# Two moves in VectorE's order: the running sum of squares in the gated unit, and the weight splits in the attention loop

## The reference, cut to what matters

```python
x = x + 0.5 * swiglu(rmsnorm(x, ffn_norm[0, 0]), ...)
h = rmsnorm(x, mix_norm[0])
# S5: scan over time, y = gelu(C s + d u), then the gated unit:
m = (y @ w_glu_v) * sigmoid(y @ w_glu_g)
x = x + m
x = x + 0.5 * swiglu(rmsnorm(x, ffn_norm[0, 1]), ...)
c, kpe = shared_kv(x, pos, ...)
x = x + 0.5 * swiglu(rmsnorm(x, ffn_norm[1, 0]), ...)
# latent attention, 16 heads, causal over the prompt; new tokens over the paged cache
s = q_lat @ c.T + q_pe @ kpe.T
p = softmax(mask(scale * s))
x = x + (heads(p @ c) @ w_uv) @ w_o
x = x + 0.5 * swiglu(rmsnorm(x, ffn_norm[1, 1]), ...)
```

## Time and profile before

| what | us |
|---|---|
| median of 3 runs | 2173.57 |
| lowest and highest | 2173.57 and 2175.39 |
| the profiled execution | 2175.88 |
| its span in the trace | 2173.9 |
| TensorE busy in the span | 2110.8 |
| VectorE busy in the span | 1065.8 |
| ScalarE busy in the span | 736.1 |

### The profile page before, as it was taken

One profiled execution on the slowest core, in us unless ns is written; L12 is line 12 of the kernel. 1 busy time (PEld: TensorE's weight loads), 2 busy tenths in 40 slices (PEclk: granted clock), 3 DMA queues, 4 the chain that ended last, 5 costly groups with the idle time before them and its releaser, 6 DMA issues.

```text
span 2173.9 us, 46399 instructions
## 1 busy us (share of the span) xinstructions
PE 2110.8 (97%) x19638; PEld 2016.3 (93%) x19638; DVE 1065.8 (49%) x1550; ACT 736.1 (34%) x1057; POOL 145.3 (7%) x246
## 2 busy tenths in 40 slices
PE   8999999998999999999999999998988999999998
PEld 7999999987999999999999999996656799999998
DVE  5453586685455454333545543345753335545422
ACT  4221232344243443223323222244543234343211
POOL 3002002030000000000000000000036100000000
PEclk9999999999999999999999999998989899999999
DMA  7232233101323323333333333221147323232332
GB/s 149 84 106 74 86 88 101 51 10 39 96 81 87 96 87 90 101 92 81 93 92 92 87 102 94 86 93 44 43 117 209 101 61 95 87 96 87 103 91 80
DMA packets 365138, 193.07 MB, mean 89 GB/s; under 512 B 42220, under 2 KB 359658, under 8 KB 365010
## 3 DMA queue, kind: packets, MB, share of 16 engines
q1 hardware_dynamic: 357952, 180.72, 29.4%
q0 software_dynamic: 5488, 9.03, 1.5%
q10 hardware_dynamic: 1570, 1.48, 0.3%
HBM read 184.23 MB, written 3.02 MB: 86 GB/s over the span
## 4 chain that ended last, share of the span: by engine, by line
PE 89%; DVE 4%; ACT 2%; SPq 2%; issue 2%; DMA 1%; ACTq 0%; DVEq 0%
PE ps L1881 76%; PE ps L1894 2%; PE ps L2428 1%; PE ps L2326 1%; PE ps L2228 1%; PE ps L2580 1%; PE ps L2459 1%; SPq L452 1%; PE ps L2200 1%; DVE wl L1222 1%; PE ps L2405 1%; SPq L454 1%; PE ps L2217 1%; DMA cb<-cache_ckv 1%; DVE stmp L482 0%
## 5 line engine op out<-in xcount | busy, mean ns | idle before, releaser
L1881 PE MATMUL ps<-xh,wh 128*128 128x260 f32 x3232 | 847.8, 283 | 6.6 <-DVE wl L1222 4.0
L1881 PE MATMUL ps<-xl,wh 128*128 128x260 f32 x3232 | 842.1, 283 | 0.0
L1881 PE MATMUL ps<-xh,wl 128*128 128x260 f32 x3232 | 651.2, 283 | 0.0
L1881 PEld LDWEIGHTS ps<-xh,wh 128*128 128x128 f32 x3232 | 610.3, 189 | 11.9 <-issue 6.4
L1881 PEld LDWEIGHTS ps<-xl,wh 128*128 128x128 f32 x3232 | 608.5, 188 | 0.0
L1881 PEld LDWEIGHTS ps<-xh,wl 128*128 128x128 f32 x3232 | 498.5, 189 | 0.0
L706 ACT ACTIVATE wh<-raw 128x1024 fp32r<-128x1024 f32 (+1 forms) x146 | 171.3, 1173 | 566.6 <-PE ps L1881 558.0
L1222 DVE TENSOR_TENSOR wl<-raw,wh 128x1024 fp32r<-128x1024 f32 (+1 forms) x156 | 213.3, 1367 | 214.0 <-ACT wh L706 200.3
L1881 PE MATMUL ps<-hh,wh 128*128 128x260 f32 x1056 | 276.2, 283 | 0.0
L724 ACT ACTIVATE wh<-raw 128x1024 fp32r<-128x1024 f32 (+1 forms) x124 | 135.5, 1093 | 414.3 <-PE ps L1881 414.3
L1881 PE MATMUL ps<-hl,wh 128*128 128x260 f32 x1056 | 275.7, 283 | 0.0
(11 more groups left out here) (452 smaller groups left out, 2269.3 us busy)
## 6 DMA issues: line engine op xcount, KB each, us to landing
raw<-ffn_w_gate SPq DMA_DIRECT2D x88, 512.0 KB, 3.8
raw<-ffn_w_up SPq DMA_DIRECT2D x88, 512.0 KB, 3.8
raw<-ffn_w_down SPq DMA_DIRECT2D x64, 704.0 KB, 4.6
cb<-cache_ckv SPq DMA_DIRECT2D x72, 128.0 KB, 2.8
cb<-cache_ckv POOLq DMA_DIRECT2D x56, 128.0 KB, 3.0
raw<-s_w_glu_v SPq DMA_DIRECT2D x8, 512.0 KB, 3.8
raw<-s_w_glu_g SPq DMA_DIRECT2D x8, 512.0 KB, 3.8
raw<-mla_w_o SPq DMA_DIRECT2D x8, 512.0 KB, 4.1
```

Source lines behind the costliest of these rows:

```text
L1881: got = mm(ps[0:width, bank + half, 0:HALF], w[par_][:, k * width:k * width + width], src[:, k0 + k, half * HALF:half * HALF + HALF], star ...
```

## The change

Two pieces of VectorE's list are put in another place; nothing is added or taken away, and the lists of all other engines stay as they are.

In the gated unit, the addition of tile d's squares stood in round d + 1, behind the two weight splits in between (`los(g0 + 2d + 4)` at the end of round d is one of them). It now stands in round d, right behind the update of x, ahead of `los(g0 + 2d + 4)`. The wait for `ss_done` is renumbered with it. In the attention loop, the split of the next weight moves from behind `weighted` and the copy `probs(i, 1)` to ahead of both.

```diff
@@ -1576,10 +1576,6 @@
             los(g0 + 2)
             for d in range(KD):
                 j = d % 2
-                if d >= 2:
-                    if d >= 3:
-                        dve.wait_ge(ss_done, SQ["glu"] + d - 2)
-                    add_squares(SQ["glu"] + d - 1)
                 if d < KD - 1:
                     los(g0 + 2 * d + 3)
                 else:
@@ -1591,6 +1587,10 @@
                 tt(x[:, d, SEQ:TOK], x[:, d, SEQ:TOK], tb[:, j, SEQ:TOK], ALU.add)
                 by_step = x[:, d, 0:SEQ].rearrange("p (c i) -> p i c", i=L)
                 tt(by_step, by_step, tb[:, j, 0:SEQ].rearrange("p (i c) -> p i c", i=L), ALU.add).then_inc(x_upd, 1)
+                if 1 <= d < KD - 1:
+                    if d >= 2:
+                        dve.wait_ge(ss_done, SQ["glu"] + d - 1)
+                    add_squares(SQ["glu"] + d)
                 if d < KD - 1:
                     los(g0 + 2 * d + 4)
             dve.wait_ge(x_upd, UPD["glu"] + KD)
@@ -1749,11 +1749,11 @@
                 more = i + 1 < NH // 2
                 if more:
                     maximum(i + 1, 0)
+                if i % 2 == 0 and more:
+                    los(PR0 + i // 2 + 2)
                 if i >= 1:
                     weighted(i - 1)
                 probs(i, 1)
-                if i % 2 == 0 and more:
-                    los(PR0 + i // 2 + 2)
                 if more:
                     maximum(i + 1, 1)
                     normalise(i + 1, 0)
```

## The result

The changed kernel took 2158.68 us in the median (2156.24 to 2162.21, 4 runs), the kernel before 2173.57 (2169.91 to 2175.39, 4 runs). The ratio is 0.9928 with the interval [0.991, 0.9946], so 15.6 us less. Two further comparisons of the same two kernels gave 0.9944 [0.9918, 0.9971] and 0.9934 [0.991, 0.9959], that is 12.2 and 14.4 us; the mean of the three is 14.1. The forecast was 11.6 us less and a range down to 2158.0; the first ratio times 2173.57 is 2157.9, outside it by 0.1, with an interval from 2154.0 to 2161.8.

The account below looks back on a forecast made before the run. TensorE, busy 97% of the span, bounds the kernel, so only its waits count. Gated unit 4.4, attention's waits 4.5 and clock 2.7 make 11.6 us: 2173.57 to 2162.0, own range 2160 to 2164, 8 times in 10 2158 to 2167.

Parts of the forecast that it names:

- The gated unit's wait, 3.0: Before line 1900: with the addition moved ahead of the split, TensorE's sum of squares starts 3.0 us earlier.
- Its limit, the seven low parts: Gated unit: VectorE's seven low parts take 5.07 us, end at 628.94 instead of 633.35, and limit the gain to 4.4 us.
- The gated unit's clock, 1.7: Behind line 1900: with the wait gone, TensorE's clock no longer falls to 1.2 GHz, worth 1.7 us.
- Attention's waits, 4 x 1.13: Before line 2428, rounds 0, 2, 4, 6: the split moved into VectorE's idle time shortens each wait by 1.13, 4.5 us.
- Attention's clock, 1.39 + 1.29: Attention rounds 0 and 4: the clock falls after the 1.59 us waits go away, 2.7 us, with 0 as other end.
- rival (a): Attention's clock terms are not there to win, or falls come elsewhere: only 8.9 us gained, 2164.7; 24%.
- rival (1) of the experiments: Both moves: the waits are the whole gain, and the clock falls are an accident of single executions; no chance given.
- Round 6, "I leave its slow stretch as it is": Attention round 6: its wait shrinks from 3.0 to about 1.85, still long, so no clock gain is counted there.
- rival (b): Attention round 6: its slow stretch shortens too, up to 3.4 us more, 2158.6; 14%.
- Does it reach the end: Behind both places: the gated unit's 4.4 us are carried, and the cache's page loads start earlier by what attention gains.
- rival (c): Cache stage: page loads set the pace behind the loop, and only the gated unit's 4.4 us arrive, 2169.2; 8%.
- rival (d): Attention: slower, the moved split waits for ScalarE's high part and holds up `xl`, `pT` and the second maximum; 2%.

Follow-up runs that it names:

- all three edits: Changed kernel plus unused matmuls filling round 6's pauses and two long page waits, and four output-product blocks among small matmuls; 0.9925 and 0.9898 against the kernel before.

## Why the prediction was right or wrong

**The gated unit's wait, 3.0: right**, 2.92 (3.08 to 0.16). **Its limit, the seven low parts: on the chain as forecast, but it took nothing off.** They took 5.00 us, 5.07 was worked out, and the whole place gave 4.41 where 4.4 was forecast. The forecast had TensorE alone 3.0 + 1.7 = 4.7 ahead and the low parts cutting that to 4.4. Measured, TensorE's own two parts are 2.92 + 1.49 = 4.41 already, and the low parts started no later behind line 1900 than with VectorE idle ahead of them. That the number came out to 0.01 is owed in part to luck: the 0.3 that the limit took off is what the two parts were too large by.

**The gated unit's clock, 1.7: the size 0.2 too large, its certainty wrong.** It is 1.49 where it falls, and it fell in six of eight executions. On the mean of executions the place gives 2.92 + 6/8 x 1.49 = 4.0.

**Attention's waits, 4 x 1.13: right to the hundredth** in all four rounds (1.59 to 0.46, 0.45 and 0.46, 2.97 to 1.84). The pause before `xl` was cover enough.

**Attention's clock, 1.39 + 1.29: right, and steadier than I feared.** In the seven profiles with waits of 1.59, round 0 took 7.09 to 7.23 in all seven, round 4 7.08 to 7.17 in five, and 5.78 and 5.80 in two; round 2 took 5.78 to 5.80 in all. With the waits at 0.45 no round ever took more than 5.80. Equal waits with unequal results went by the round far more than by the execution. So rival (a), that these terms are not there to win, was wrong, and with it rival (1) of the experiments: on the mean 2.3 of the 2.7 us are.

**Round 6, "I leave its slow stretch as it is": the step that failed.** It was a term of the sum, set to 0, and it measures 1.3 us in five of six profiles. The argument was that 1.85 is still longer than a wait that had been followed by a fall. That looked at the wait alone. What the rows show is that the stretch holds two pauses. Before, the clock fell around the first; now, in five of six profiles, it falls only behind the second, and the work between the two runs at full speed. The argument also left out the rounds ahead: with their waits short, even the full wait of 2.98 was left at full speed. The rival (b) had it as up to 3.4; what it gave was between the two.

**Does it reach the end: right.** From the second product of the next block to line 2493, the first small matmuls of attention, it is 849.78 us before and 849.77 after, so the gated unit's gain arrives whole. The cache stage took 96.15 and 95.56 us before, 97.14, 94.96 and 94.35 after. The +0.99 of the profiled pair is within what it does by itself, so rival (c) falls. Nothing of rival (d) was seen.

**The sum.** With the measured sizes, as means over the executions, it is 4.0 + 4.5 + 2.3 + 1.5 = 12.3 us against 11.6. The traces say much the same: attention as a whole took 119.84 and 120.25 us in the two profiles of the kernel before and 111.22, 111.35 and 111.27 in the three after, 8.8 less, where the waits, both falls (the two profiles of before had them both) and round 6 in these three make 4.5 + 2.7 + 1.3 = 8.5.

**The range.** The rest is the lower end. With round 6 in the sum the forecast would have been 12.9 to 13.1 us less, 2160.7 to 2160.5; that the first comparison then fell below the range, by 0.1 us, is chance. The mean of three comparisons, 14.1 us, has an uncertainty of nearly 3 us by the three intervals, and 12.3 lies within it. The first comparison, with four runs a side and an interval of 7.8 us from end to end, came out 1.5 above that mean. The range had allowed 4 us below the forecast for rival (b) and the runs' spread together, the latter counted with 0.6. Two stretches that the change does not touch show why that was too little.

The profiles of the changed kernel and of its unedited copy, timeline of TensorE where the first small matmuls of attention stand. First the changed kernel, with the window behind them, then the copy with its own:

```profile
1485.50 3.74 PE L2493 MATMUL ps<-qq,ukT 64*128 64x8 f32 x64
```

```profile
1490.00:1495.00 5.00, 4.45 (x21) 2.10 (x20) 1.92 (x2) 2.59 (x3) 0.00 (x0) 1.00 0.01 3
```

```profile
1486.40 4.73 PE L2493 MATMUL ps<-qq,ukT 64*128 64x8 f32 x64
```

```profile
1490.00:1495.00 5.00, 5.00 (x27) 4.05 (x26) 0.69 (x1) 0.58 (x4) 0.00 (x0) 0.50 0.00 0
```

The granted clock is 1.00 in one execution and 0.50, the level of 1.2 GHz, in the other, and from line 2493 to attention's second pair it is 16.21 and 19.90 us. The second place is the tail. The changed kernel, then its copy:

```profile
1710.07 4.47 PE L2643 MATMUL ps<-tb,ob 128*128 128x32 f32 x32
...
1716.45 6.85 PE L2652 MATMUL ps<-sq,cb 128*128 128x16 f32 x32
```

```profile
1712.61 3.65 PE L2643 MATMUL ps<-tb,ob 128*128 128x32 f32 x32
...
1717.61 3.92 PE L2652 MATMUL ps<-sq,cb 128*128 128x16 f32 x32 [0.19 <-DVE sq L1831]
```

From the first row to the first sum of the last block it took 24.46 and 20.08. Over all 18 profiles this tail was 20.0 to 20.1 five times and 24.4 to 26.0 eleven times, in kernels of every kind (25.99 and 20.04 in the two of the kernel before), and 21.6 in both profiles with all three edits. The first of the two stretches varies too (from the gated unit's end to attention it is 865.98 to 870.4 in the 17 profiles in which it can be read, 867.4 and 869.5 in those of the kernel before). If both extremes meet, that moves a single execution by 4.4 + 6.0, some 10 us (an estimate from these lengths), whatever the kernel, and it can move a median of four runs by a part of that.

Two more estimates of what the change is worth come from the spans. As they are, the two of the kernel before are 2173.9 and 2172.5, the three of the changed one 2160.1, 2158.3 and 2159.7: 13.8 us less on the mean. With both stretches taken out, 1280.5 and 1283.0 against 1269.7, 1268.5 and 1267.7 are left: 13.1 us less. Of these 13.1, 3.7 lie between the update of tile 6 and the second product, 8.8 in attention, and 0.7 ahead of the one and in the cache stage, which the change does not touch and which vary by more than that in one kernel (the cache stage from 94.35 to 97.14 in the changed one). So these five traces put the change at 12.4 to 13.1 us, where the corrected sum has 12.3 and the comparisons 14.1 with their 3 us of uncertainty.

## What to carry to other kernels

An operation whose input is ready belongs ahead of one that still waits, if the engine runs its list in order; how much the move gives is read from the wait of the bound engine, and what is late next is worked out before it is summed. A wait shorter than before can be worth more than its own length if the clock used to fall in it, so a slow stretch with several pauses is to be valued pause by pause, not set to nothing because one pause stays long. And before a range is drawn, look for stretches that run at either clock from one execution to the next: here they can, by estimate, move a single execution by 10 us, nearly as much as the change.

## What the runs showed of the hardware

The same idle time does not always bring the clock down. A wait of 3.07 us was followed by a granted clock of 0.50 in most executions and of 1.00 in others; a wait of 1.59 was always followed by a fall in round 0, mostly in round 4 and never in round 2, in seven profiles of four kernels. So it is not chance alone, and the length of the wait is not all that counts; that it is what TensorE did before the wait is argued from this and was not tested by itself. The clock also falls without idleness: 64 matmuls of 64x8 and 32 of 128x32 and 128x16, issued one behind the other with TensorE counted as busy throughout, are where the clock fell in the two stretches above in some executions and not in others (that their small size is the reason is not shown), and it stayed low through the first full-size matmuls behind them (0.42 us a row instead of 0.28). Where matmuls whose result nobody uses filled a wait, the work behind them ran at full speed: in round 6 in three of three profiles (in one of six without them), and behind the first long page wait in three of three (in none of the changed kernel's three); where 2.16 us of a page wait stayed open, it did not.
